# The order of weight splits, gain rows and hidden pieces in a fused two-block kernel, at five places

## The reference

```
first_block, for each of 2 layers:
    x = x + 0.5 * swiglu(rms_norm(x, ffn1_norm[l]), ffn1_gate[l], ffn1_up[l], ffn1_down[l])
    h = rms_norm(x, mix_norm[l]) @ w_in[l]
    x = x + concat(pool, moba attention, dilated attention, conv)(h) @ w_out[l]
    x = x + 0.5 * swiglu(rms_norm(x, ffn2_norm[l]), ffn2_gate[l], ffn2_up[l], ffn2_down[l])
x = rms_norm(x, final_norm)

second_block, for each of 2 layers, on x and (in layer 0) on a context of 256 tokens:
    xm, cm = modulate(h, ...), modulate(hc, ...)          # rms norm, scale and shift per channel
    y = even_mixer(xm, cm, ...)  or  odd_mixer(xm, cm, ...)   # layer 0, layer 1
    h = h + gt_m * rms_norm(y, g_post_m)
    f = conv_ffn(modulate(h, ...), w_up[l], conv_w[l], conv_b[l], w_down[l])
    h = h + gt_f * rms_norm(f, g_post_f)
    (layer 0: the same for the context hc)
```

## Time and profile before

| | |
|---|---|
| median of 3 runs | 2073.74 us (2073.28 to 2075.41) |
| profiled execution | 2073.74 us |
| its span, first to last instruction | 2071.2 us |
| PE busy, PEld busy | 1977.9 us (95%), 1750.2 us (85%) |
| DVE busy, ACT busy, POOL busy | 1183.5 us (57%), 930.0 us (45%), 13.5 us (1%) |
| granted TensorE clock, mean | 0.975 |
| DMA | 320.81 MB, mean 155 GB/s |

### The profile page before, as it was taken

One profiled execution on the slowest core, in us unless ns is written; L12 is line 12 of the kernel. 1 busy time (PEld: TensorE's weight loads), 2 busy tenths in 40 slices (PEclk: granted clock), 3 DMA queues, 4 the chain that ended last, 5 costly groups with the idle time before them and its releaser, 6 DMA issues.

```text
span 2071.2 us, 31855 instructions
## 1 busy us (share of the span) xinstructions
PE 1977.9 (95%) x13586; PEld 1750.2 (85%) x13586; DVE 1183.5 (57%) x1555; ACT 930.0 (45%) x1310; POOL 13.5 (1%) x17
## 2 busy tenths in 40 slices
PE   6999978999999999799999998999999999998998
PEld 6998857999799988599988885988888879678997
DVE  4545775544554458754456436565555356757774
ACT  5334534433443354453345436443333254565553
POOL 0000000000000000000000010000000000000000
PEclk9999978999999999799999999999999999999999
DMA  7765544666556654556544321132223222114552
GB/s 284 260 227 183 168 147 154 224 224 232 195 196 231 225 183 163 183 206 244 203 143 143 124 70 52 62 102 102 82 102 102 96 88 82 62 44 141 183 187 97
DMA packets 45499, 320.81 MB, mean 155 GB/s; under 512 B 5040, under 2 KB 5168, under 8 KB 6960
## 3 DMA queue, kind: packets, MB, share of 16 engines
q1 hardware_dynamic: 38592, 270.09, 37.6%
q10 hardware_dynamic: 6768, 48.69, 6.4%
HBM read 317.72 MB, written 1.05 MB: 154 GB/s over the span
## 4 chain that ended last, share of the span: by engine, by line
PE 88%; DVE 6%; ACT 3%; issue 2%; DMA 1%; POOLq 0%; POOL 0%; SPq 0%; DVEq 0%; ACTq 0%
PE ps L516 86%; DVE s_wl L1843 2%; PE ps L831 1%; DVE s_big L2113 1%; ACT s_wh L1196 1%; PE ps L694 0%; DMA s_ca<-in_c_all 0%; PE ps L671 0%; PE ps L793 0%; DVE s_X L2003 0%; ACT s_xh L1196 0%; DMA s_big<-in_bias 0%; DVE s_tmp L1984 0%; DVE s_tmp L2318 0%; DVE s_xl L1843 0%
## 5 line engine op out<-in xcount | busy, mean ns | idle before, releaser
L1843 DVE TENSOR_TENSOR s_wl<-s_raw,s_wh 128x2048 fp32r<-128x2048 f32 x215 | 492.4, 2291 | 363.0 <-ACT s_wh L1196 362.8
L516 PE MATMUL ps<-s_xh,s_wl 128*128 128x256 f32 (+1 forms) x2208 | 677.0, 307 | 23.0 <-DVE s_wl L1843 22.4
L516 PE MATMUL ps<-s_xh,s_wh 128*128 128x256 f32 (+1 forms) x2208 | 669.5, 303 | 0.0
L516 PE MATMUL ps<-s_xl,s_wh 128*128 128x256 f32 (+1 forms) x2208 | 669.4, 303 | 0.0
L1196 ACT ACTIVATE s_wh<-s_raw 128x2048 fp32r<-128x2048 f32 x215 | 409.6, 1907 | 198.4 <-PE ps L516 198.0
L516 PEld LDWEIGHTS ps<-s_xh,s_wl 128*128 128x128 f32 x2208 | 424.4, 192 | 42.2 <-DVE s_wl L1843 22.8
L516 PEld LDWEIGHTS ps<-s_xl,s_wh 128*128 128x128 f32 x2208 | 424.6, 192 | 15.8 <-issue 0.5
L516 PEld LDWEIGHTS ps<-s_xh,s_wh 128*128 128x128 f32 x2208 | 424.2, 192 | 15.8
L516 PE MATMUL ps<-s_wh,s_hl 128*128 128x512 f32 (+1 forms) x608 | 233.0, 383 | 2.3 <-DVE s_hl L1923 2.3
L516 PE MATMUL ps<-s_wh,s_hh 128*128 128x512 f32 (+1 forms) x608 | 230.7, 380 | 0.0
L516 PE MATMUL ps<-s_wl,s_hh 128*128 128x512 f32 (+1 forms) x608 | 230.7, 379 | 0.0
(11 more groups left out here) (236 smaller groups left out, 2355.0 us busy)
## 6 DMA issues: line engine op xcount, KB each, us to landing
s_big<-in_w_ada ACTq DMA_DIRECT2D x46, 1024.0 KB, 6.5
s_raw<-in_ffn_gate SPq DMA_DIRECT2D x44, 1024.0 KB, 6.6
s_raw<-in_ffn_up SPq DMA_DIRECT2D x44, 1024.0 KB, 5.0
s_raw<-in_ffn_down SPq DMA_DIRECT2D x44, 1024.0 KB, 5.0
s_raw<-in_w_up SPq DMA_DIRECT2D x44, 1024.0 KB, 4.9
s_raw<-in_w_down SPq DMA_DIRECT2D x22, 1024.0 KB, 4.9
s_raw<-in_w_in SPq DMA_DIRECT2D x18, 1024.0 KB, 4.9
s_raw<-in_w_in_ab SPq DMA_DIRECT2D x10, 1024.0 KB, 5.0
```

The lines of the kernel that those rows point to most:

```text
L516: return pe.matmul(o, lhsT, rhs, start=start, stop=stop, skip_group_check=True)
L1843: dve.tensor_tensor(wide(wl, u), raw[:, u % SLOTS, :].rearrange("p (k n) -> p k n", k=8), f32(wide(wh, u)), SUB).then_inc(*w_low.tick(u))
```

## The change

Five places of the order are changed; no operation is added or taken away.

1. In the second feed-forward block of layer 1, `beside_down[n]` comes before the hidden piece n + 1 instead of behind it, on ACT and on DVE.
2. In the even attention, the `gains` of ("m", 0, 0) are made before `value(0)` on PE and ACT; the diagonals on DVE stay where they were.
3. There too, the splits given free by units `w_in_ab` 8 and 9 (`w_out_ab` 1 and 2) leave steps 4 and 6 of the loop: on ACT they stand right behind the copies of each value product, on DVE the first stands before the loop and the second in step 2.
4. The split given free by `w_down` 10 (`w_qkv` 4) stands at the end of the convolution block, ahead of `bound_high` and `bound_low` of stream 0, instead of behind them.
5. In the odd attention, the `gains` of ("m", 1, 0) are made at step 20 of the value projection instead of behind it, and the split given free by `w_qkv` 5 stands before step 2 of the loop instead of in step 6.

```
 PE, even:
+                gains(("m", 0, 0), (4, 5))
                 value(0)
                 for n in range(len(H.units) + 3):
                     if n == 2:
-                        gains(("m", 0, 0), (4, 5))
                         value(1)
                     attend(H, n)
 PE, odd:
                 tokens(u[5], [2, 3], [("odd", "v", 0), ("odd", "v", 1)], (0, 1, 2, 3),
-                       aside={1: step3, 9: step4, 17: step5, 23: lambda: attend(H, 0), 25: lambda: attend(H, 1)})
+                       aside={1: step3, 9: step4, 17: step5, 20: lambda: gains(("m", 1, 0), (0, 1)), 23: lambda: attend(H, 0), 25: lambda: attend(H, 1)})
                 freed[2], freed[3] = copied["odd", "v", 0], copied["odd", "v", 1]
-                gains(("m", 1, 0), (0, 1))
 ACT, ffn (DVE the same with hid_low):
                 for n in range(11):
+                    if n in beside_down:
+                        beside_down[n]()
                     if n >= 1 and n + 1 < 11:
                         hid_high(s, n + 1, hid, n + 1, 0, hidden[s, n + 1])
-                    if n in beside_down:
-                        beside_down[n]()
                     if n:
                         high_after(unit[f"{tag}_down", 11 * l + n - 1])
 ACT, even:
                         act.activation(Ve[:, 2 * n:2 * n + 2, 256 * i:256 * i + 256], pair(ps[6 + n][:, :]),
                                        ACT.Copy).then_inc(*copied.tick(("even", "v", i, n)))
+                    high_after(u[8 + i])
...
+                gains(("m", 0, 0), (4, 5))
                 value(0)
-                def between(n):
-                    if n == 2:
-                        gains(("m", 0, 0), (4, 5))
-                        value(1)
-                    if 3 <= n < 7:
-                        gated_high(n - 3)
-                    if n in (4, 6):
-                        high_after(u[6 + n // 2])
                 for n in range(len(H.units) + 3):
-                    attend(H, n, lambda: between(n))
+                    attend(H, n, (lambda: value(1)) if n == 2 else (lambda: gated_high(n - 3)) if 3 <= n < 7 else None)
 ACT, conv_ffn and odd (DVE the same with low_after and bound_low):
-                    if q == streams[-1] and (j < 10 or l):
+                    if q == streams[-1]:
                         high_after(unit["w_down", 11 * l + j])
...
                 bound_high(P[0], pre_mixer(1), 0, 1, 2, 3)
-                high_after(unit["w_down", 10])
 ACT, odd:
                 copy("q3", 0, 1, "q_g", ("odd", "q", 3))
+                gains(("m", 1, 0), (0, 1))
                 attend(H, 0)
                 attend(H, 1)
...
-                gains(("m", 1, 0), (0, 1))
+                high_after(u[5])
                 for n in range(2, len(H.units) + 3):
                     attend(H, n)
-                    if n == 6:
-                        high_after(u[5])
 DVE, even:
                 gain_diagonals(("m", 0, 0), 0, 1)
+                low_after(u[8])
                 for n in range(len(H.units) + 3):
...
                     attend(H, n)
-                    if n in (4, 6):
-                        low_after(u[6 + n // 2])
+                    if n == 2:
+                        low_after(u[9])
 DVE, odd:
                 gain_diagonals(("m", 1, 0), 0, 1)
                 attend(H, 0)
                 attend(H, 1)
+                low_after(u[5])
                 for n in range(2, len(H.units) + 3):
                     attend(H, n)
-                    if n == 6:
-                        low_after(u[5])
```

More of the change, by code:

```diff
@@ L2485, in odd @@
                 bound_low(P[0], pre_mixer(1), 0, 1, 2, 3)
-                low_after(unit["w_down", 10])
                 for b in range(3):
```

1 line of the change is left out of this document (removed).

## The result

The changed kernel took 2089.32 us (median of 4 executions, 2088.93 to 2090.43), the kernel before 2073.77 us (4 executions on the same chip, 2073.28 to 2075.41): ratio 1.0075, 95% interval 1.0057 to 1.0092. It is 15.6 us slower; 2088.1 was forecast. The profiled execution took 2087.8 us with a span of 2085.8, 14.6 more than before. No engine's busy total shows the loss.

The account below looks back on a forecast made before the run. The prediction took PE's matmuls to bound the kernel (88% of the chain), DVE or ACT only where PE waits. Four stretches, 3.5 + 2.5 + 5.0 + 3.4 = +14.4 us on 2073.7, gave 2088.1 us, range 2081 to 2095.

Parts of the forecast that it names:

- C: Down projection, second feed-forward block of layer 1: PE waits before steps 4 to 7, +3.5 us (1.5 to 6).
- A: Even attention: 6.0 us wait before the gain product, 2.4 slower clock, 5.9 returned by splits and masks: +2.5 us.
- D: Passage from convolution block to odd mixer: the early split delays stream 0's eviction and PE, +5.0 us (4 to 6).
- B: Odd attention: first transposes 6.2 us later, 5.1 given back in the loop, 2.3 for slower clock: +3.4 us.
- R1: Rival, faster: both attentions return to PE's beat, the even one gaining 12.5 us; 2064.6 us, chance 0.03.
- R2: Rival, no change: early gain rows cost nothing in either attention, down-projection waits hidden behind PE; 2072.1 us, chance 0.05.
- R3: Rival: repeated waits in down projection (up to 7 us) and even loop (4) lower PE's clock; 2097 us, chance 0.10.
- R4: Rival: early splits return more than forecast, bringing the even attention to -6 us; 2079.6 us, chance 0.08.
- two meetings: Even attention: two GpSimd mask additions fall into DVE's dense part, 0.38 us each, some 0.8 us, inside the bounds.

Follow-up runs that it names:

- a_splits: Kernel before with only the two output-weight splits of the even attention moved early, gain rows left in place: 2067.55 us, ratio 0.9979.
- b_late: Kernel before with the split in step 6 of the odd attention moved behind the whole loop: 2069.22 us, ratio 0.9973.
- only_a: Kernel before with only the change's even-attention edits, early gain rows and early splits (items 2 and 3): 2076.51 us, ratio 1.0014.
- a_gains: Kernel before with only the early gain rows of the even attention, splits left in place: 2081.12 us, ratio 1.0046.
- only_d: Kernel before with only the split given free by w_down 10 moved ahead of stream 0's bound_high and bound_low (item 4): 2078.17 us, ratio 1.0022.
- a_late: Kernel before with the even attention's first output-weight split early, the second behind the whole loop, gain rows unchanged: 2064.44 us, ratio 0.9949.
- only_b: Kernel before with only the odd-attention edits, early gain rows and split before step 2 (item 5): 2079.05 us, ratio 1.0025.

## Why the prediction was right

Each of the four mechanisms was there, where it was said to be. The terms:

| term | predicted | in the changed kernel |
|---|---|---|
| C: PE's four waits, steps 4 to 7 | +3.5 | step 7 later by 3.46 against the stretch's start; stretch +3.1 |
| A: wait before the gain product | +6.0 | 5.94 |
| A: clock behind it | +2.4 | 12 x 0.24 = 2.9 |
| A: returned by splits and masks | -5.9 | 3.0 - 5.9 - 2.9 = -5.8; a_splits alone -5.6 (median -5.1) |
| D: PE's next product | +5.0 | wait 11.57 instead of 6.54, +5.03; stretch +4.6 |
| B: wait before the gain product | 2.1 | 1.84 |
| B: first transposes | +6.2 | 1802.96 - 1785.99 - 10.39 = +6.6 |
| B: wait before them, clock behind it | 4.5, +2.3 | 4.44, 12 x 0.23 = 2.8 |
| B: returned | -5.1 | 4.1 - 6.6 - 2.8 = -5.3; b_late alone -5.1 |
| sum | +14.4 | +14.8, and 15.6 by the medians |

(10.39 is by how much the root product ahead of B came later.) The waits are the solid part of this table: they are read directly, and the kernels with one part each show them again to 0.1 us. The two terms that say "returned" are what is left when the others are taken off, so of their own they confirm nothing; a_splits and b_late do.

The price of the clock is the soft part. I had taken it from the earlier trace rows, one execution, where 0.80 was the grant behind one wait; behind the new waits of A and B it was 0.76 and 0.77 in the changed kernel, 0.5 us more each than forecast. But the same wait of 5.94 us was followed by 0.86 in only_a and by 0.77 in a_gains, that of 11.57 by 0.84 in the changed kernel (against 0.80 before, the 0.4 by which D's stretch fell short of PE's wait) and by 0.76 in only_d, whose stretch is +5.5. One such fall thus costs anything from 12 x 0.14 = 1.7 to 12 x 0.24 = 2.9 us, and A's stretch has its own spread of up to 1.7 us. That 14.4 came within 0.4 of the sum of the stretches is therefore in part luck; the four waits and their sizes are not.

In B the prediction adds 1.7 us to the wait without deriving it, and then takes 3.5 of the 3.8. The last copy of the value projection on ACT came 1797.49 - 1783.32 - 10.39 = 3.8 us later. The 1.7 is real: it is the gain product itself, 1.8 us on PE before (1783.12 to 1784.93), which used to stand behind that copy's product and now stands ahead of it.

The rivals. R1 needed DVE's work in the even loop to shrink; DVE is busy 33.08 of 34.20 us there, and even with both splits out (a_late) the whole stretch gained 8.6, not 12.5. R2 needed the early gain rows free: they cost 7.4 and 2.0. R3 needed the repeated short waits to bring the clock down: in C four waits of up to 1.43 left it at 1.00, and the changed kernel's even loop has 0.95 with a wait of 1.66. Falls behind short waits exist, though: behind that of 1.8 in only_b, and in the even loop of the kernel before, where the 12 us behind a wait of 1.83 were granted 0.85. Each cost under 2 us over those 12 (12 x 0.14 and 12 x 0.15), not the 4 to 7 of R3. R4 had the return nearly right (it is -5.6 without the gain rows) but not the wait's price.

On DVE and GpSimd the prediction allowed 0.38 us for each of two meetings. One took place; during the first addition DVE had no instruction with both inputs in SBUF. Timelines of GpSimd and DVE in the changed kernel:

```profile
1258.37 1.28 POOL L2637 TENSOR_TENSOR s_big<-s_big,s_cb 128x512 f32<-128x512 f32 x1 [9.89 <-DMA s_big<-in_bias]
1260.45 1.27 POOL L2637 TENSOR_TENSOR s_big<-s_big,s_cb 128x512 f32<-128x512 f32 x1 [0.80 <-DMA s_big<-in_bias]
...
1260.86 0.41 DVE L2026 TENSOR_TENSOR s_xl<-ps,s_xh 128x256 fp32r<-128x256 f32 x1
1261.19 1.07 DVE L2379 TENSOR_TENSOR s_xl<-s_big,s_xh 128x512 fp32r<-128x512 f32 x1
...
1265.31 0.68 DVE L2379 TENSOR_TENSOR s_xl<-s_big,s_xh 128x512 fp32r<-128x512 f32 x1
```

The instruction with both inputs in SBUF took 0.39 more than its twin 4 us later, and it began 0.53 before the addition's recorded end. The one ahead of it, with one input in PSUM, kept its 0.41. The Trainium skill, "SBUF — State Buffer", section "SBUF: two separate sides", says that a DVE instruction with two SBUF inputs is fully blocked while a GpSimd instruction that reads SBUF has the shared pair of ports. By that rule the price is what is left of the addition, at most 0.53 here, not its length; the rows fit that. The instruction with a PSUM input is not of the kind that the rule names, and it kept its time.

## What to carry to other kernels

In hand-ordered programs, price a moved step by when its operand is written by the other engine, not by when its own engine has time: the early gain rows in A and B made PE arrive at a wait that their old place had covered, and in C, D and B a piece that nobody needed soon was put ahead of the one that PE waited for. Such a piece belongs where its engine has time and PE doesn't wait for what stands behind it. Moved out of the loop, the two splits of A gave 8.6 us (5.6 with one of them left in step 2); moved behind the dense work, those of B and D gave 5.1 and 2.2, where the change's places cost time. A repeated round of three engines is as long as its chain across them, so read whose start waits for whose end before changing the order on one: with two pieces swapped on ACT alone, the round fell from 7.13 to 5.72 us. And price a fall of the clock by a range from several executions, not by one window.

## What the runs showed of the hardware that was not expected

The same program doesn't meet its lower clock at the same places each time. The kernel before took 2066.6 to 2076.3 us in 31 executions, and up to 4.5 us of difference arose in profiled executions before the first changed instruction; this, not the edits, is what blurs single runs of this kernel. Behind the wait of 6.5 us at the passage, which ten of the kernels have unchanged, the next 12 us were granted 0.80 (before) to 0.88 (only_b). And a wait of 1.8 us at the same place was followed by a mean of 0.86 over 12 us in only_b, but by 1.00 in the changed kernel.
